# One layer of a hybrid trunk with experts on one core: a ring of sixteen weight buffers for twelve, and the first expert's latents fetched as whole rows

## What is computed

```python
def expert_choice_moe(h, w_router, w_gate, w_up, w_down):
    cap = max(1, EC_CAPACITY_FACTOR * N // N_EXPERTS)      # 64 latents, 16 context tokens
    aff = jax.nn.softmax((h @ w_router).astype(jnp.float32), axis=-1)
    gates, idx = lax.top_k(aff.transpose(0, 2, 1), cap)
    def one(hb, gb, ib):
        xe = hb[ib]                                        # (16, cap, 1024)
        hid = jax.nn.silu(xe @ w_gate) * (xe @ w_up)       # (16, cap, 2048)
        ye = (hid @ w_down) * gb[..., None]
        return jnp.zeros_like(hb).at[ib.reshape(-1)].add(ye.reshape(-1, D))

def trunk_layer(x, cond, ...):
    x = x + gate1 * token_mixer(rms_norm(x) * (1 + scale1) + shift1)
    h2 = rms_norm(x) * (1 + scale2) + shift2
    x = x + gate2 * expert_choice_moe(h2, ...)
```

## Time and profile before

| | us |
|---|---|
| median of 3 runs | 1711.03 |
| lowest, highest | 1709.94, 1712.18 |
| the profiled execution | 1713.24 |
| its span | 1711.3 |
| first expert's gate begins (in the span) | 700.50 |
| last expert's w_down begins | 1674.66 |

### The profile page before, as it was taken

How to read it: one execution, slowest core, us unless ns; L and a number is a source line. 1 busy time by engine, 2 the same in 40 slices (tenths; PEclk the granted TensorE clock), 3 DMA queues, 4 the chain that set the end, 5 groups by cost and what they waited for, 6 DMA issues and landing times.

```text
span 1711.3 us, 32043 instructions
## 1 busy us (share of the span) xinstructions
PE 1666.0 (97%) x13900; PEld 859.0 (50%) x13900; DVE 565.0 (33%) x974; ACT 343.3 (20%) x702; POOL 284.9 (17%) x238
## 2 busy tenths in 40 slices
PE   6999999999999989899999999999999999999997
PEld 3767778778888868333333333333333333333332
DVE  2797627347676684311011011011011101101101
ACT  4533222246666733100000000000000000000000
POOL 1364404000010000101210220220220121121011
PEclk9999999999999999899999999999999999999998
DMA  9446644323132044799999999999999999999994
GB/s 337 164 155 213 216 171 136 103 79 97 41 97 79 33 176 158 286 421 412 412 421 414 413 418 417 413 413 422 412 413 422 413 413 421 414 413 421 414 414 168
DMA packets 122198, 507.34 MB, mean 296 GB/s; under 512 B 13100, under 2 KB 35076, under 8 KB 72984
## 3 DMA queue, kind: packets, MB, share of 16 engines
q1 hardware_dynamic: 111856, 484.80, 70.8%
q0 software_dynamic: 9536, 21.52, 4.5%
q10 hardware_dynamic: 744, 0.15, 0.0%
HBM read 487.02 MB, written 19.42 MB: 296 GB/s over the span
## 4 chain that ended last, share of the span: by engine, by line
PE 90%; DVE 3%; DMA 3%; issue 1%; POOL 1%; ACT 1%; SPq 0%; DVEq 0%; ACTq 0%; POOLq 0%
PE banks L2139 56%; PE banks L1761 8%; PE banks L1763 7%; PE banks L1762 7%; PE banks L1991 2%; PE banks L1978 2%; PE banks L1902 2%; DMA raw_k<-in_w_down_e 1%; PE banks L1786 1%; DMA raw<-in_w_ada 1%; PE banks L1805 1%; PE banks L1940 1%; POOL qk_swp L1654 0%; DVE var L1157 0%; PE banks L2088 0%
## 5 line engine op out<-in xcount | busy, mean ns | idle before, releaser
L2139 PE MATMUL banks<-raw,xe 128*32 128x512 f32 x2304 | 255.8, 596 | 2.3 <-DVE xe L1443 2.3
L1610 DVE TENSOR_TENSOR hid<-banks,sg 128x512 f32<-128x512 f32 x48 | 31.1, 673 | 599.9 <-PE banks L2139 599.9
L1761 PE MATMUL banks<-w_hi,h_hi 128*128 128x512 f32 x560 | 225.8, 403 | 3.2 <-DVE w_lo L1090 2.9
L1763 PE MATMUL banks<-w_lo,h_hi 128*128 128x512 f32 x560 | 219.6, 392 | 0.0
L1762 PE MATMUL banks<-w_hi,h_lo 128*128 128x512 f32 x560 | 218.9, 391 | 0.0
L1726 POOL DMA_INDIRECT out<-yeg_c,idx_c x64 | 83.5, 1305 | 811.6 <-DVE yeg_c L1595 797.0
L1069 ACT ACTIVATE sg<-banks 128x512 f32<-128x512 f32 x48 | 25.2, 597 | 904.8 <-PE banks L2139 904.8
L2139 PEld LDWEIGHTS banks<-raw,xe 128*32 128x32 f32 x2304 | 75.0, 111 | 168.8 <-issue 166.2
L2139 PE MATMUL banks<-raw_x,hT 128*32 128x512 f32 (+1 forms) x1536 | 127.4, 486 | 3.4 <-DMA raw_x<-in_w_down_e 3.4
L2139 PE MATMUL banks<-raw_k0.5_54,xe 128*32 128x512 f32 x1152 | 129.8, 592 | 0.0
L2139 PE MATMUL banks<-raw_x,xe 128*32 128x512 f32 x1152 | 126.7, 592 | 0.0
(11 more groups left out here) (249 smaller groups left out, 1899.9 us busy)
## 6 DMA issues: line engine op xcount, KB each, us to landing
raw<-in_w_gate_e SPq DMA_DIRECT2D x48, 1024.0 KB, 20.6
raw<-in_w_up_e SPq DMA_DIRECT2D x48, 1024.0 KB, 21.9
raw_x<-in_w_down_e SPq DMA_DIRECT2D x48, 1024.0 KB
raw_k0.5_54<-in_w_gate_e SPq DMA_DIRECT2D x32, 1024.0 KB, 20.4
raw_k1.5_55<-in_w_gate_e SPq DMA_DIRECT2D x32, 1024.0 KB
raw_x<-in_w_up_e SPq DMA_DIRECT2D x32, 1024.0 KB
raw_k<-in_w_up_e SPq DMA_DIRECT2D x32, 1024.0 KB, 22.1
raw_k1.5_55<-in_w_down_e SPq DMA_DIRECT2D x32, 1024.0 KB
```

Source lines behind the costliest of these rows:

```text
L1610: nc.vector.tensor_tensor(hid[:, part, :].rearrange("p (f a j) -> p f a j", j=STRIP, a=2), in_turn(bank(3 + part)), in_turn(sg[:, part, :] ...
L1761: nc.tensor.matmul(ps, hi, wh, start=first, stop=False)
L1763: return nc.tensor.matmul(ps, hi, wl, start=False, stop=last)
L2139: done = nc.tensor.matmul(out(i), left(i), right(i), start=first, stop=last)
```

## The change

The ring has 16 buffers: two on the addresses of attention's old slots (NRAWE and NRAWE + 1), and two new ones, `raw_w`, over places where the second norm's tiles lie (x2, and h2T and what is behind it). 16 doesn't divide 24, so an even expert's chunk i and an odd one's are in different buffers, and PE's and SP's loops run two experts a turn. Chunk 3 is loaded once the latents' stores have landed, 4 to 7 behind W(NL, 0), 8 to 12 behind W(NL, 1), 13 to 15 behind L(NL).

The first expert's latents are fetched by one indirect DMA of 64 whole rows of 4 KB into `xrow`; its index is a copy of `older`, so G isn't needed for it. PE turns the rows by 32 small matmuls with the identity, four strips of 32 columns for each k, into banks 7 and 6, and DVE reads them from there. This step, E(0) on PE, with the eight filling transposes ahead of it, stands ahead of L(NL) and P(NL), and G has moved behind these. PE runs one k tile (`AHEAD_OF_A`, three matmuls) of W(NL, 0) ahead of A(0) and not four. The later experts' gathers are as before.

```diff
-NOWN = 8
+NOWN = 10
-EXPERT_SLOT = [2, 0, 1] + [NRAWE + i for i in range(4, 8)] + list(range(NRAW, NRAWE)) + [NRAWE + 2, NRAWE + 3]
+EXPERT_SLOT = [2, 0, 1, NRAWE + 8] + [NRAWE + i for i in range(4, 8)] + list(range(NRAW, NRAWE)) + [NRAWE + i for i in (2, 3, 0, 1, 9)]
...
-    steps = [("W", NL, 0), ("W", NL, 1), ("D", 0)] + [("K", i) for i in range(CAP_L // 8)] + [("J", 0), ("J", 1), ("G", 0)]
-    steps += [("V", 0), ("V", 1), ("N", NL, 0), ("X", NL, 0), ("N", NL, 1), ("X", NL, 1), ("R", NL), ("S", NL), ("L", NL), ("P", NL)]
-    return steps + [("E", 0), ("U", 1), ("A", 1), ("K", CAP_L // 8), ("K", CAP_L // 8 + 1), ("F", 0), ("E", 1)]
+    steps = [("W", NL, 0), ("W", NL, 1), ("D", 0)] + [("K", i) for i in range(CAP_L // 8)] + [("J", 0), ("J", 1)]
+    steps += [("V", 0), ("V", 1), ("N", NL, 0), ("X", NL, 0), ("N", NL, 1), ("X", NL, 1), ("R", NL), ("S", NL), ("E", 0), ("L", NL), ("P", NL), ("G", 0)]
+    return steps + [("U", 1), ("A", 1), ("K", CAP_L // 8), ("K", CAP_L // 8 + 1), ("F", 0), ("E", 1)]
...
+AHEAD_OF_A = 1
...
-P2_BANK = {("L", NL, 0): 5, ("A", 1, 0): 6, ("F", 0, 0): 7}
+P2_BANK = {("L", NL, 0): 5, ("G", 0, 0): 3, ("A", 1, 0): 5, ("F", 0, 0): 4}
+ROW_BANK = (7, 6)
...
+    def slot_of(odd, i):
+
+        return EXPERT_SLOT[(EC * odd + i) % NEX]
...
+    xrow = place("xrow", [CAP_L, D], offset=WORK)
...
+    idx_row = place("idx_row", [CAP_L, E], U32)
...
+    raw_w = [place(f"raw_w{i}", [P, CK, CW], offset=offset) for i, offset in enumerate((WORK + 4 * 2 * COLS_X * KT, WORK + 4 * NT * D + 12 * D))]
...
+            sp.wait_ge(x2_out, 16 * NL)
+            load_expert(3)
             sp.wait_ge(p2_done, P2.index(("W", NL, 0)) + 1)
-            for i in range(3, 7):
+            for i in range(4, 8):
                 load_expert(i)
             sp.wait_ge(p2_done, P2.index(("W", NL, 1)) + 1)
-            for i in range(7, 10):
+            for i in range(8, NEX - 3):
                 load_expert(i)
             store_tile(NL)
-            sp.wait_ge(xg_in, 16 * (PARTS_X - 1))
-            for i in range(10, NEX):
+            sp.wait_ge(p2_done, P2.index(("L", NL, 0)) + 1)
+            for i in range(NEX - 3, NEX):
                 load_expert(i)
+            sp.wait_ge(xrow_in, 16)
...
-            expert_loads(0, False)
-            with sp.Fori(1, E - 1) as e:
-                expert_loads(e, False)
-            expert_loads(E - 1, True)
+            expert_loads(0, 0, False)
+            with sp.Fori(1, E - 2, 2) as e:
+                expert_loads(e, 1, False)
+                expert_loads(e + 1, 0, False)
+            expert_loads(E - 1, 1, True)
...
+            def first_latents_modulated(half):
+
+                k, own = slice(4 * half, 4 * half + 4), slice(0, CAP_L)
+                dve.wait_ge(xrow_done, half + 1)
+                rows = bank(ROW_BANK[half])[:, 0:CAP_L * 4].rearrange("p (k t) -> p k t", k=4)
+                nc.vector.tensor_tensor(xm[:, k, own], rows, amp_x[:, k, own], ALU.mult).then_inc(xrow_mul, 1)
+                dve.wait_ge(xrow_mul, half + 1)
                 nc.vector.tensor_tensor(xe[:, k, own], xm[:, k, own], shift_x[:, k, own], ALU.add).then_inc(xe_ready, 1)
...
                     dve.wait_ge(older_ready, 1)
+                    nc.vector.tensor_copy(idx_row[:, :], older[0:CAP_L, :]).then_inc(row_ready, 1)
...
+            pool.wait_ge(row_ready, 1)
+            pool.indirect_dma_start(xrow[:, :], None, xn_d[0], bass.IndirectOffsetOnAxis(ap=idx_row[:, 0:1], axis=0)).then_inc(xrow_in, 16)
             pool.wait_ge(idxg_ready, 1)
-            wait_emptied(pool, ("G", 0, 0))
-            gather(0, range(PARTS_X - 1))
...
-                    output_part(BEFORE[step], 0, CK)
+                    output_part(BEFORE[step], 0, AHEAD_OF_A if what == "A" else CK)
...
+                elif what == "E" and t == 0:
+                    meanwhile(MEANWHILE["E"], ROW_BANK[0])
+                    pe.wait_ge(xrow_in, 16)
+                    for k in range(KT):
+                        for i in range(4):
+                            c = QUARTER * i + STRIP * k
+                            last = nc.tensor.matmul(bank(ROW_BANK[k // 4])[STRIP * i:STRIP * i + STRIP, CAP_L * (k % 4):CAP_L * (k % 4) + CAP_L], xrow[:, c:c + STRIP],
+                                                    ident[0:CAP_L, 0:CAP_L], start=True, stop=True)
+                        if k % 4 == 3:
+                            last.then_inc(xrow_done, 1)
...
-            meanwhile(MEANWHILE["E"], 7)
             for step in (("X", NL, 1), ("W", NL, 1), ("G", 0, 0)):
                 wait_emptied(pe, step)
...
-            expert(0, True, False)
-            with pe.Fori(1, E - 1) as e:
-                expert(e, False, False)
-            expert(E - 1, False, True)
+            expert(0, 0, True, False)
+            with pe.Fori(1, E - 2, 2) as e:
+                expert(e, 1, False, False)
+                expert(e + 1, 0, False, False)
+            expert(E - 1, 1, False, True)
```

More of the change, by code:

```diff
@@ L648, in wait_read, with expert_loaded @@
                 eng.wait_ge(piece_done, PIECE_AT[b, NT - 1] + 1)
-        def expert_loaded(e, i):
-            slot = EXPERT_SLOT[i % NEX]
-            return raw_in[slot], e * (16 * EC // NEX) + 16 * (RAW_BEFORE[slot] + i // NEX + 1)
+        def expert_loaded(e, odd, i):
+            slot, turn = slot_of(odd, i), (EC * odd + i) // NEX
+            return raw_in[slot], e * (16 * EC // NEX) + (16 * (RAW_BEFORE[slot] + turn + 1) - odd * (16 * EC // NEX))
         def wait_emptied(eng, step):
@@ L766, in _, with expert_loads @@
                 sp.dma_start(gate2_c[STRIP * i:STRIP * i + STRIP, :], gate_d[1, 1:2, c].broadcast_to([STRIP, CW // 2])).then_inc(gate2_in, 16)
-            def expert_loads(e, last):
+            def expert_loads(e, odd, last):
                 for i in range(EC):
@@ L1490, in _ @@
                     for half in range(2):
-                        tokens_modulated(0, half, range(PARTS_X - 1))
+                        first_latents_modulated(half)
                 elif what == "E":
@@ L1619, in expert @@
                     for half in range(2):
-                        tokens_modulated(e + 1, half, range(PARTS_X))
+                        tokens_modulated(e + 1, half)
                 gated_output(e, first, last)
@@ L1712, in gather @@
             def gather(e, groups):
-                if e >= 1:
-                    pool.wait_ge(xt_done, 2 * e)
+                if e >= 2:
+                    pool.wait_ge(xt_done, 2 * e - 2)
                 if e == 1:
@@ L2068, in stage_step @@
                 elif what == "W":
-                    output_part(step, CK if step in BEFORE.values() else 0, KT)
+                    output_part(step, AHEAD_OF_A if step == BEFORE["A", 0] else CK if step in BEFORE.values() else 0, KT)
                 elif what == "X":
@@ L2171, in first_gate, with expert @@
                         stage_step(("F", 0))
-                    pe.wait_ge(*expert_loaded(0, i))
+                    pe.wait_ge(*expert_loaded(0, 0, i))
                     for part in range(2):
-                        hidden_part(0, part, i, expert_buffer(i))
+                        hidden_part(0, part, i, expert_buffer(0, i))
                 pe.wait_ge(xec_ready, 1)
                 for i in range(KT):
-                    hidden_part(0, 2, i, expert_buffer(i)).then_inc(chunk_read, 1)
-            def expert(e, first, last_e):
+                    hidden_part(0, 2, i, expert_buffer(0, i)).then_inc(chunk_read, 1)
+            def expert(e, odd, first, last_e):
                 if first:
@@ L2196, in expert @@
                     if f % 2 == 0:
-                        pe.wait_ge(*expert_loaded(e, ES + f // 2))
-                    last = down_context(f, down_rows(f))
+                        pe.wait_ge(*expert_loaded(e, odd, ES + f // 2))
+                    last = down_context(f, down_rows(odd, f))
                 if last_e:
@@ L2203, in expert @@
                     if not last_e and f >= AHEAD and f % 2 == 0:
-                        pe.wait_ge(*expert_loaded(e, ES + f // 2))
-                    last = down_latent(f, down_rows(f))
+                        pe.wait_ge(*expert_loaded(e, odd, ES + f // 2))
+                    last = down_latent(f, down_rows(odd, f))
                     if not last_e:
                         if f >= AHEAD:
-                            last = down_context(f, down_rows(f))
+                            last = down_context(f, down_rows(odd, f))
                         if f % 2 == 1:
```

37 lines of the change are left out of this document (19 added, 18 removed).

## The result

The changed kernel takes 1747.65 us (median of 4 runs, 1746.09 to 1748.29) where the kernel before takes 1711.61 on the same chip (1709.94 to 1712.87): a ratio of 1.021, 95% interval 1.0192 to 1.0228. It is 36 us slower; 1703.4 was predicted, with a range up to 1716. The profiled execution ran 1746.09 us with a span of 1744.3.

What follows compares the result with a forecast made beforehand. PE was taken to set the pace, with DMA having nothing to spare; -9.3 us for sixteen buffers and +1.6 for the front gave -7.7, applied to the median 1711.03: 1703.4 us, range 1700 to 1716.

Steps and rivals of the forecast that it cites:

- The jump back (part 1): PE's loop over experts, unrolled by two for sixteen buffers: six jumps back, taken as 0, bounds 0 to 42 us.
- Rival 1: PE's loop: ten packets of code do not stay, PE stands still at each jump; 1719.8 or 1711.6 us; chance 0.28.
- the quiet gather's 2.73 us: A gather at 711.97 to 714.70 with little else moving, issue to use; rival 1's price for each jump.
- The code's load on the DMA engines (part 1): Expert loop: seven turns of ten packets, 1.1 MB more to move, 2.8 us at 416 GB/s.
- the lead of 3.2 us: Last expert: the last chunk lands 959.0 us after first buffer reuse, PE needs it at 962.2, so no waits.
- the sum had 959.0: Expert loads: 368 chunks remaining after the first buffer reuse, at 2.606 us each, take 959.0 us.
- rival 3: Last expert still waits: ring does not fill or loads slow with more waiting; 1707 to 1710 us; chance 0.10.
- The tail, -9.3: Last expert with sixteen buffers: context half gains 8.1 us, latents' half 1.2 us, as waits and clock fall go.
- The front, +1.6: Router to first expert: first gate matmul at 702.1 instead of 700.50; bounds -0.7 to +13.3 us.
- rival 2: First latents' small row matmuls cost the logits' rate, +13.3 us instead of +1.6, 1715.0 us; chance 0.07.
- J 1.8 us sooner instead of 0.85: Transposes after the top-64, before the first expert: start near 685.7 instead of 686.55, gain 0.85 us.
- rival 4: Front: whole rows and small matmuls faster than taken and lift the clock; gate at 699, 1700 us; chance 0.05.

Runs made afterwards that it cites:

- the hinted kernel: Changed kernel, loop of two experts kept, one instruction per turn announcing PE's jump back so its target can be fetched ahead; 1716.92 us, ratio 1.0039.
- quiet engines: Changed kernel with every load after the first sixteen fetching only a quarter of its columns, DMA share 0.4, output different; one run, 1730.07 us.
- the written-out kernel of before: Kernel before, ring of twelve and front untouched, only PE's fourteen middle experts written out instead of looped; 1721.83 us against 1709.97, ratio 1.0065.
- the changed kernel written out: Changed kernel with PE's fourteen middle experts written out instead of looped two a turn; 1716.12 us against 1710.15, ratio 1.0039.
- the kept chunks: Kernel before, ring of twelve, loop of one expert, four extra buffers holding the last expert's last four w_down chunks; 1703.18 us against 1709.97, ratio 0.9962.
- the jumps are mended: Changed kernel without the pauses at PE's jumps back: middle experts written out (1716.12 us), or loop kept with the jump announced ahead (1716.92 us).
- part 2 alone: Kernel before with only the affinities' transposes moved sooner, three matmuls ahead of them; 1708.3 us, ratio 0.9994.
- the quiet rows: Kernel before with the changed front, ring of twelve, only two instead of seven weight loads ahead of the row gather; 1711.24 us, ratio 1.0014.
- Front: Kernel before, ring of twelve, with both front changes: affinities' transposes sooner, first latents fetched as whole rows; 1712.43 us, ratio 1.0015.
- the ring alone: Kernel before with the ring of sixteen, PE's middle experts written out, front as it was; 1714.6 us, ratio 1.0023.
- three kept chunks: Kernel before with extra buffers holding only the last expert's w_down chunks 21 to 23, ring of twelve; 1704.88 us, ratio 0.9975.

## Why the prediction was wrong, step by step

**The jump back (part 1), priced at 0.** This is the step that failed: a term put at nothing that measured 41.7 us in the loop, 27.5 of them PE standing still and some 12.5 the low clock behind the pauses, and about 30 us in the time, because the pauses also let the DMA engines catch up. "No fetch of code shows as a PE gap in the straight stretches" was true and did not bear on a jump: in a straight stretch the next packet is known ahead, at an unhinted jump it is not, and the hinted kernel shows that this is the whole difference. The bounds stood in the text (0 to 6.98 us a jump, 42 us in all), the packets of the earlier trace rows told only that five had been kept, and the range was closed at 2 us a jump all the same. Rival 1 named the mechanism and was given 0.28. Its price, the quiet gather's 2.73 us, is what the pause measures with quiet engines (2.63 to 2.94); in this loop the engines are saturated, for which the loaded row was the right one, and the clock's fall behind each pause (1.6 to 2.9 us) was in no bound. The rule of the Trainium skill (Runtime: NRT & Kernel Launch, Instruction fetch mechanics), that a taken branch outside the window stalls for a fetch, was right here, with 4.5 to 4.7 us. Its window of two pages was not: the old body is five packets long, and no packet of code was fetched from 924 to 1544 while it looped; the prediction took that for agreement, and for the window the measurement decides.

**The code's load on the DMA engines (part 1), priced at 2.8 us.** 10.9 us by the written-out kernel of before (last chunk 1699.40 for 1687.91, less 0.6 us by which its first reuse came later, 719.02 for 718.45). The prediction divided bytes by 416 GB/s, as if a packet were spread over sixteen engines like a chunk. A packet takes one engine about 1.0 us (0.5% of 16 x 124 us for ten), and if eight share them that is 66 x 1.0 / 8 = 8.3 us. The remaining 2.6 us of the 10.9 stay unexplained; a packet may hold up its engine for longer than its own record. So the lead of 3.2 us was a lag: in the changed kernel written out, the last of the 368 chunks lands 970.5 us after the first reuse (1690.89 for 720.42), where the sum had 959.0, and PE wants it after 962.8. Without added code the sum's 959 holds: with the kept chunks the DMA engines are done near 1677, some 957 us after the first reuse at 720.01. That is rival 3, with the price of its own reason wrong fourfold, and it is what remains when the jumps are mended: 1716, not 1703.

**The tail, -9.3.** Right in mechanism and size where the chunks do arrive: -9.3 with the kept chunks. The -9.1 of the changed kernel is luck: its pauses gave the chunks the time, and with the jumps mended nothing of it is left. First reuse near 720: 718.93. The packets: over 100 were to tell that the code does not stay, and 122 came.

**The front, +1.6.** The first gate matmul came 34.89 us after the router's last sixteen, +1.6 as forecast, 702.1 in the time of the trace of before, but by terms that cancel. Landing 7.7 us instead of 4.5 (taken between the quiet row and the loaded one, while the nine loads asked for ahead of it spoke for the loaded one); row matmuls 1.9 us instead of 4.0, near their lower bound, so rival 2 is out (its 1715 us also counted a late landing; with the landing that the sum took it would have been 1713); J 1.8 us sooner instead of 0.85 (1.1 with part 2 alone), as the clock came back earlier in W. The row matmuls did not lift the clock, so rival 4 is out: it was 0.97 to 1.00 while PE waited for the rows (690 to 693.4), 0.50 during them and on to 703; with the quiet rows it was 0.50 from 690 through 702. Over many runs the front costs 2.6 us (1.0 to 4.3). One term was missing: the gather of the context was taken "as before" while four more loads were queued ahead of it. PE waits for it 1.2 us in the changed kernel, 2.9 with the kept chunks.

**Do the pieces add up?** Front +2.6, ring without its code -6.5, code +11.1: +7.2 us, where the written-out kernel measured +6.7 (4.3 to 9.1). Without the front it is +4.6, where the ring alone measured +3.9 (2.1 to 5.8). With the jumps' 30 us the whole makes 37, for 36 measured; that last step is no check of its own, as the 30 come from the same runs.

## What to carry to other kernels

A loop body is a resource: before unrolling a loop on an engine, count its instructions in packets of code, and if they are more than the trace shows being kept, price every jump at a loaded fetch plus the clock that it costs, or hint the jump. Where the DMA engines are saturated, code that is fetched again competes with the data, and by the plateau it does so unevenly: the engine that is last sets when a chunk lands. Extra buffers need not lengthen a ring whose length divides the loop; holding the last turn's data in them gave the same 9.3 us at the end for no code at all.

## What the runs showed of the hardware that was not expected

- A loop of 1,280 recorded PE instructions an expert stays in the engine (no packets for it in the trace of before), one of 2,560 does not: 11 or 12 packets came in each 124 us of the changed kernel, and the pause is 4.5 to 4.7 us at a DMA share of 1.02, 2.6 to 2.9 us at 0.4. With the hint it is under 0.1 us a turn. Bodies between these two sizes were not tried.
- Straight code is not free either. The Trainium skill (Runtime: NRT & Kernel Launch, Instruction fetch mechanics) calls the crossing into the next block "mostly hidden" and has kernels prefer full unrolling. For PE's own supply that holds here: the written-out experts show no gap for code. For the kernel it does not: 66 packets beside saturated loads cost 11 us (7.7 to 14.5).
- After 66 more packets of code the DMA share falls in two steps, with some 12 to 14 us at 0.51 between them (estimated from the stretches of 4 us).
- A gather of 64 rows of 4 KB lands in 3.9 us on quiet engines and in 7.7 to 7.9 with seven to nine weight loads asked for ahead of it.
- In one profiled run with the front of before (three kept chunks) the J transposes came 3 us nearer to the router's last sixteen than in the others (16.2 us for 19.3), because the clock came back earlier inside W. A microsecond read at the front from one profile is worth little; the medians decide.
